# A two-block transformer kernel on one core: hi/lo operands side by side, and a turned triangular inverse

## The reference

```python
h = rms_norm(x, norm_mix_pre); proj = h @ w_in
o_sb = stick_breaking_attention(q, k, v); o_rw = rwkv7_time_mix(p_rw, ...)
merged = gates[..., :D] * (o_sb @ w_sb_out) + gates[..., D:] * (o_rw @ w_rw_out)
x = x + rms_norm(merged @ w_o, norm_mix_post)
h = rms_norm(x, norm_ffn_pre)
x = x + rms_norm((silu(h @ w_ffn_gate) * (h @ w_ffn_up)) @ w_ffn_down, norm_ffn_post)
# second block
x = x + hybrid_mixer(rms_norm_2(x, g_mix), w_in, conv_w, ...)
x = x + memory_cross_attention(rms_norm_2(x, g_xattn), rms_norm_2(mem, g_mem), ...)
x = x + squared_relu_mlp(rms_norm_2(x, g_mlp), w_up, w_down)
out = rms_norm_2(x, g_final)
```

## Time and profile before

| what | value |
|---|---|
| median of three runs | 852.21 us |
| the profiled execution, its own time | 853.91 us |
| its span in the trace | 852.0 us |
| mean granted clock of TensorE | 0.995 |
| busy: PE, DVE, ACT | 839.8, 546.1, 394.4 us |
| mean DMA rate | 165 GB/s |

### The profile page before, as it was taken

One profiled execution on the slowest core, in us unless ns is written; L12 is line 12 of the kernel. 1 busy time (PEld: TensorE's weight loads), 2 busy tenths in 40 slices (PEclk: granted clock), 3 DMA queues, 4 the chain that ended last, 5 costly groups with the idle time before them and its releaser, 6 DMA issues.

```text
span 852.0 us, 16571 instructions
## 1 busy us (share of the span) xinstructions
PE 839.8 (99%) x7276; PEld 773.3 (91%) x7276; DVE 546.1 (64%) x606; ACT 394.4 (46%) x457; POOL 5.9 (1%) x8
## 2 busy tenths in 40 slices
PE   9999999999999999999999999999999999999997
PEld 8989889898989999999999989988998999999996
DVE  5998755546788655555557656595754765566554
ACT  6652331366367434343447354446544533344432
POOL 0000010000000000000000000000000000000000
PEclk9998999999999999999999999999999999999999
DMA  9845513131674665646553754536433465555531
GB/s 299 282 150 177 167 54 102 54 99 53 241 244 132 198 199 196 194 151 200 194 198 100 246 170 136 175 124 206 176 103 123 140 228 174 180 193 183 178 133 49
DMA packets 97002, 140.62 MB, mean 165 GB/s; under 512 B 2480, under 2 KB 79408, under 8 KB 96944
## 3 DMA queue, kind: packets, MB, share of 16 engines
q1 hardware_dynamic: 96512, 139.36, 50.0%
q10 hardware_dynamic: 432, 0.39, 0.2%
HBM read 138.69 MB, written 1.05 MB: 164 GB/s over the span
## 4 chain that ended last, share of the span: by engine, by line
PE 88%; DVE 6%; ACT 2%; issue 2%; DMA 2%; SPq 0%; ACTq 0%; DVEq 0%
PE PS L427 86%; DMA raw<-in_w_in_dram 2%; DVE wlo L1627 2%; PE PS L530 1%; ACT whi L1201 1%; DVE rw L1689 1%; DVE diff L1686 0%; DVE stg L1684 0%; DVE Gm L1781 0%; ACT st L1201 0%; PE PS L673 0%; PE PS L1037 0%; DVE cs L1706 0%; DVE wlo L1664 0%; DVE krs L1719 0%
## 5 line engine op out<-in xcount | busy, mean ns | idle before, releaser
L1627 DVE TENSOR_TENSOR wlo<-raw,whi 128x2048 fp32r<-128x2048 f32 x122 | 279.4, 2291 | 136.8 <-ACT whi L1201 136.5
L1201 ACT ACTIVATE whi<-raw 128x2048 fp32r<-128x2048 f32 (+1 forms) x130 | 241.2, 1858 | 181.3 <-PE PS L427 177.7
L427 PE MATMUL PS<-xh,whi 128*128 128x256 f32 x1136 | 322.4, 287 | 0.9 <-ACT xh L1201 0.7
L427 PE MATMUL PS<-xh,wlo 128*128 128x256 f32 x1136 | 317.2, 284 | 0.1
L427 PE MATMUL PS<-xl,whi 128*128 128x256 f32 x1136 | 315.2, 284 | 0.0
L427 PEld LDWEIGHTS PS<-xh,whi 128*128 128x128 f32 x1136 | 217.9, 193 | 5.9 <-issue 3.3
L427 PEld LDWEIGHTS PS<-xh,wlo 128*128 128x128 f32 x1136 | 217.2, 193 | 0.3 <-DVE wlo L1664 0.3
L427 PEld LDWEIGHTS PS<-xl,whi 128*128 128x128 f32 x1136 | 215.7, 193 | 1.1
L427 PE MATMUL PS<-whi,fh 128*128 128x512 f32 x216 | 84.4, 391 | 0.0
L427 PE MATMUL PS<-wlo,fh 128*128 128x512 f32 x216 | 84.4, 391 | 0.0
L427 PE MATMUL PS<-whi,fl 128*128 128x512 f32 x216 | 84.1, 389 | 0.0
(11 more groups left out here) (310 smaller groups left out, 1045.0 us busy)
## 6 DMA issues: line engine op xcount, KB each, us to landing
raw<-in_w_in_dram SPq DMA_DIRECT2D x32, 1024.0 KB, 5.3
raw<-in_w_up_dram SPq DMA_DIRECT2D x16, 1024.0 KB, 5.3
raw<-in_w_down_dram SPq DMA_DIRECT2D x16, 1024.0 KB, 4.9
raw<-in_w_ffn_gate_dram SPq DMA_DIRECT2D x11, 1024.0 KB, 5.3
raw<-in_w_ffn_up_dram SPq DMA_DIRECT2D x11, 1024.0 KB, 5.4
raw<-in_w_ffn_down_dram SPq DMA_DIRECT2D x11, 1024.0 KB, 5.0
raw<-in_w_kv_mem_dram SPq DMA_DIRECT2D x8, 1024.0 KB, 5.4
raw<-in_w_o_dram SPq DMA_DIRECT2D x4, 1024.0 KB, 8.0
```

The lines of the kernel that those rows point to most:

```text
L427: return nc.tensor.matmul(o, l, r, start=start, stop=stop, **kw)
L1201: return nc.scalar.activation(o, i, f, **kw)
L1627: V.tensor_tensor(wlo[u % RING][:], raw[u % RING][:], whi[u % RING][:].bitcast(f32), ALU.subtract) \
```

## The change

`xh` and `xl` lie side by side for each k in one tile `xhl` (and `memhl`), so that one matmul can stream both: 512 columns. In 63 of the units by features (`by_feature_wide`: 4 of `U_QK`, 8 of `U_G`, 2 of `U_KM`, 20 of the first feed-forward, 3 of `U_QK2`, 8 of `FILL2`, 3 of `U_QM`, 15 of the last feed-forward), a tile f is 8 matmuls `whi` with `xhl` of 512 columns, then 8 matmuls `wlo` with `xh` of 256 columns. The left half of a bank holds whi*xh + wlo*xh, the right half whi*xl; a unit fills two banks. ACT copies the right halves out (`second_halves`, by unit, or by tile in `FILL2` and `U_QM`), DVE adds the left halves (`summed`), and then multiplies by the norm factors in SBUF. The units of the stages `U_QK`, gates, `FILL2` and `U_QM` use fewer bank pairs than before; the gate units all use banks 0 and 1 and wait for the sum of the unit before.

The inverse no longer updates `TT` by a product. `join` forms only the update of `Tm`, `lower` streams only the 32 columns that the level needs, and a new `turned(v)` forms the new columns of `TT` by a matmul of `Tm` with the identity (32 columns), which DVE copies out in `lower_out` of the next level. The pairs and transposes that stood between (`pairs(eN, eX)`, `tokens(rw, 8)`) use banks 6 and 7, and the products behind the inverse change their order.

The maximum and reciprocal of `krs` move ahead of the eight instructions that end in `k_mod`.

```diff
+            def by_feature_wide(u, both, banks, later=0, before=None, between=None, amidst=None, first=None):
+                n = units[u][1]
+                wh, wl = split(u, n, later)
+                for f in range(2):
+                    if before:
+                        before(f)
+                    fs = slice(f * P, (f + 1) * P)
+                    o = bank(banks[f])
+                    for k in range(KD):
+                        if amidst:
+                            amidst(f, k)
+                        mm(o, wh[:, k, fs], both[:, k].rearrange("p a t -> p (a t)"), k == 0, False, skip_group_check=True)
+                    for k in range(KD):
+                        last = mm(o[:, 0:SEQ], wl[:, k, fs], both[:, k, 0], False, k == KD - 1, skip_group_check=True)
...
             def lower(v):
+                n = HD // 2
                 pe.wait_ge(sem("t_ready"), v)
-                pe.wait_ge(sem("tt_ready"), v)
-                for c, tt, s_, h, b, l, r in out_of(lambda c, tt, s_: XT[half(c), c ^ tt, s_, :], lambda c, tt, s_: Tm[half(c), c ^ tt, s_, :]):
-                    last = mm(PS[h, b * 512 + s_ * HD:b * 512 + (s_ + 1) * HD], l, r, True, True)
+                if v == 1:
+                    pe.wait_ge(sem("tt_ready"), 1)
+                else:
+                    turned(v - 1)
+                if v == 6:
+                    return
+                for c, tt, s_, h, b, l, r in out_of(lambda c, tt, s_: XT[half(c), c ^ tt, s_, :],
+                                                    lambda c, tt, s_: halves(Tm[half(c), c ^ tt, s_, :], v, 0)):
+                    last = mm(PS[h, b * 512 + s_ * n:b * 512 + (s_ + 1) * n], l, r, True, True)
                 last.then_inc(sem("g_mm"), 1)
+            def turned(v):
+                n = HD // 2
+                for c, tt, s_, h, b, l, r in out_of(lambda c, tt, s_: Tm[half(c), c ^ tt, s_, :],
+                                                    lambda c, tt, s_: halves(C("ident")[half(c), half(c)], v, 1)):
+                    last = mm(PS[h, b * 512 + 256 + s_ * n:b * 512 + 256 + (s_ + 1) * n], l, r, True, True)
+                last.then_inc(sem("turn_mm"), 1)
...
             def gate_unit(i):
                 before(i)
-                pe.wait_ge(sem("out_evac"), i + 10)
-                by_feature(U_G[i], xh, xl, (i + 11) % 2, None, lambda f: amid(i))
+                if i == 0:
+                    pe.wait_ge(sem("summed"), halved("qk", 4))
+                else:
+                    pe.wait_ge(sem("summed"), halved("gate", i))
+                by_feature_wide(U_G[i], xhl, (0, 1), between=lambda: amid(i))
                 behind(i)
...
+            def second_halves(dst, banks):
+                return A_(dst, tiles(banks)[:, :, 1], ACT.Copy)
...
+            def summed(dst, banks):
+                return V.tensor_tensor(dst, tiles(banks)[:, :, 0], dst, ALU.add)
...
                 if i == 5:
+                    dve.wait_ge(sem("kk_sd"), 1)
+                    link(V.tensor_scalar(krs[:], krs[:], 1e-12, None, ALU.max))
+                    V.reciprocal(krs[:], krs[:]).then_inc(sem("kk_rs"), 1)
+                if i == 5:
                     for j in range(NPAIR):
...
-                if i == 5:
-                    dve.wait_ge(sem("kk_sd"), 1)
-                    link(V.tensor_scalar(krs[:], krs[:], 1e-12, None, ALU.max))
-                    V.reciprocal(krs[:], krs[:]).then_inc(sem("kk_rs"), 1)
...
             def mlp(i, n=0):
                 later = FF2_BODY * n
+                if i:
+                    act.wait_ge(sem("units_used"), U_M["u", i] + 1 + FF2_STEP * n)
+                    if i >= 2:
+                        act.wait_ge(sem("mlp_hi"), i - 1 + later)
+                        act.wait_ge(sem("mlp_sq"), i - 1 + later)
+                    second_halves(pair(fa[i % 2]), MLP_BANKS[i % 2]).then_inc(sem("mlp_second"), 1)
```

More of the change, by code:

```diff
@@ L249, in bank, with halved, tiles @@
             return PS[:, b * 512:(b + 1) * 512]
+        HALVED = {"qk": 4, "gate": 8, "km": 2, "qk2": 3, "fill": 16, "qm": 6}
+        def halved(kind, n):
+            return sum(HALVED[o] for o in list(HALVED)[:list(HALVED).index(kind)]) + n
+        def tiles(banks):
+            a, b = banks
+            return PS[:].rearrange("p (b h t) -> p b h t", b=8, h=2)[:, a:b + 1:b - a]
         def C(name):
@@ L712, in join @@
             def join(v):
                 pe.wait_ge(sem("g_ready"), v)
+                pe.wait_ge(sem("tt_ready"), v)
                 n = HD // 2
[L715 to L728, removed]
+                for c, tt, s_, h, b, l, r in back_to(lambda c, tt, s_: TT[half(c ^ tt), c, s_, :],
+                                                     lambda c, tt, s_: halves(Gm[half(c ^ tt), c, s_, :], v, 0)):
+                    last = mm(PS[h, b * 512 + s_ * n:b * 512 + (s_ + 1) * n], l, r, True, True)
@@ new lines, in behind @@
+            def behind(i):
+                if i == 0:
+                    pe.wait_ge(sem("pair_ready"), 1)
+                    pairs(eX, kk, "pair_mm")
+                elif i < 6:
+                    join(i)
+                    if i in (2, 3):
+                        pe.wait_ge(sem("pair_ready"), 4)
+                        pe.wait_ge(sem("tok_ready"), i - 1)
+                        for j in range(NPAIR):
+                            last = nc.tensor.transpose(PS[:, 7 * 512 + j * P:7 * 512 + (j + 1) * P],
+                                                       rw[:, 8 + j, (i - 2) * P:(i - 1) * P], C("ident"))
+                        last.then_inc(sem("tok_T"), 1)
+                elif i == 6:
@@ L2119, in mem_queries @@
             def mem_queries(i):
-                dve.wait_ge(sem("units_used"), U_QM[i] + 1)
-                V.tensor_tensor(qm[:, 2 * i:2 * i + 2, :], two(i % 2 if i else 2), spread(rs), ALU.mult).then_inc(sem("qm_evac"), 1)
+                if i == 0:
+                    dve.wait_ge(sem("units_used"), U_QM[i] + 1)
+                    V.tensor_tensor(qm[:, 0:2, :], two(2), spread(rs), ALU.mult).then_inc(sem("qm_evac"), 1)
+                    return
+                for f in range(2):
+                    dst = qm[:, 2 * i + f, :]
+                    dve.wait_ge(sem("second"), halved("qm", 2 * i + f - 1))
+                    V.tensor_tensor(dst, bank(f)[:, 0:SEQ], dst, ALU.add).then_inc(sem("summed"), 1)
+                    dve.wait_ge(sem("summed"), halved("qm", 2 * i + f - 1))
+                    last = V.tensor_tensor(dst, dst, rs, ALU.mult)
+                last.then_inc(sem("qm_evac"), 1)
             dve.wait_ge(norm_sem("n4", "rs"), nth("n4", "rs", 1))
```

358 lines of the change are left out of this document (230 added, 128 removed).

## The result

The changed kernel takes 841.79 us (median of four executions, 841.16 to 842.34) where the kernel before took 852.23 us beside it: ratio 0.9878, 95% interval 0.986 to 0.9895. It is 10.4 us faster. The forecast was 835.2 us, so the sign was right and 6.6 us of the 17.0 are missing; the time also lies above the range's end of 841.

The account below looks back on a forecast made before the run. PE's own stream was taken to bound the kernel. Wide operand 10.6 + inverse 4.7 + stretch up to the gate stage 2.3 - new waits 0.6 = 17.0 us off the median 852.21: 835.2 us, range 832.5 to 841.

Parts of the forecast that it names:

- Term 1: Wide units: fewer, wider matmuls save 0.18 us a unit; 59 units behind the first stage give 10.6 us (10.0 to 12.4).
- deduction for changes of width: Wide units: about two more narrow-to-wide changes a unit at 0.02 us each, 0.04 us off the saving.
- best case of 0.21 us a unit: Wide units: sixteen pairs of 768 columns, each 0.347 us instead of 0.360, save 0.21 us a unit.
- Term 2: Inverse: three 32-column blocks a level replace the old products, 14.4 us instead of 19.2; 4.7 us taken as saving.
- Term 4: New waits on added copies and sums, gate stage, state part and feed-forwards: mostly covered, 0.6 us lost.
- Term 3: Up to the gate stage: krs wait and slow clock go, DVE's gn_pre then limits; 2.3 us earlier (1.5 to 3).
- signs that the prediction had named: Trace marks for each part: matmul distances, block times, clock and logits start, PE's waits on copies and sums under 2 us.
- (B): Before the gate stage: PE's 2 us stand drops the clock, costing 1.7 to 3.4 us; 838 us, chance 0.25.
- (C): Inverse: bound by its chain over DVE, so shorter matmuls only lengthen waits and its saving is lost; 840 us, chance 0.09.
- (D): Wide units: fixed cost per matmul is not saved, gain 2.4 us or less; 843 to 846 us, chance 0.06.
- (E): Loops: weight supply turns late behind the added copy and add, kernel slower; 860 us at 1 us per turn, chance 0.05.
- (F): Whole kernel: losses from new waits add up to the whole gain; 851 to 854 us, chance 0.03.

Follow-up runs that it names:

- x4: The changed kernel with each 512-column matmul of the wide units issued as two of 256 columns, copies and sums kept: 853.55 us, ratio 1.0007.
- x7: x3 with wide and narrow matmuls in turn for each k, 32 changes of width a unit instead of 4: 839.84 us.
- x6: x3 with the inverse of the kernel before, its pairs and transposes back in their old places and banks: 841.87 us.
- x1: The changed kernel with DVE's key_sum set ahead of the lo that stood before it, for both key units: 836.85 us, ratio 0.981.
- x8: The kernel before once more, unchanged, for a second trace: 852.51 us over 12 executions, the traced one 852.32 us.
- x5: The kernel before with only the maximum and reciprocal of krs moved ahead of the k_mod instructions: 850.58 us, ratio 0.9976.
- x9: The changed kernel once more, unchanged, for a second trace and more executions: 841.34 us, ratio 0.9868.
- x2: The changed kernel with DVE's lo for a gate unit's weights moved behind the group norm preparations: 840.47 us, ratio 0.9858.
- x3: The changed kernel with both the edit of x1 and the edit of x2: 835.05 us, ratio 0.9786.

## Why the prediction was wrong, point by point

- **What bounds the kernel:** right. PE sets the pace, and removing its instructions moved the time.
- **Term 1, the wide operand:** right in mechanism and near in size. x4 gives 11.8 us for the 63 units against 11.3 forecast; that 2.0 us of it are stalls and 1.0 us is hidden by waits makes the match of the medians partly luck, but 0.191 us a unit in the last feed-forward is free of both. A turn of the last feed-forward takes (822.05 - 689.73) / 12 = 11.03 us (the starts of two down units, twelve turns apart), as forecast. The deduction for changes of width was too large (x7), and the best case of 0.21 us a unit was not reached either. Between the parts of dilated attention and of memory attention the units saved only 0.10 and 0.07 us in place of 0.18. The trace of x4 splits this: narrow matmuls cost 1.07 and 0.33 us there (0.13 and 0.11 a unit), and x4, which has the added copies and sums without the saving, takes 0.29 and 0.13 us more than before.
- **Term 2, the turned inverse:** right in sum for a partly wrong reason. The whole is worth 5.5 to 6.8 us (x6), forecast 4.7. The products give 3.7 of it and not 4.8, the shorter waits for `Gm` 1.5, and 0.5 is a stall that no wait explains. Term 4 had put the inverse's waits at 0.2 us more; they became less. It also had 0.4 us more for `St`, whose waits stayed at 0.5 us.
- **Term 3, up to the gate stage:** the start at 94.50 was forecast at 95.3, the wait for `gn_pre` at 2 and measured at 1.75 us. The size of the clock's share was right where it happened: 3.1 us forecast, 3.05 measured between two traces of the same kernel. The sum of DVE's work and idle time was 0.8 us too pessimistic.
- **Term 4, new waits: this is the step that failed.** It sums the new waits to a loss of 0.6 us. It names the gate stage, the state part and both feed-forwards, and finds, in the feed-forwards, a whole unit of 5.5 us between a sum and the reuse of its banks. `U_KM[1]` and the second unit of `U_QK2` share banks 0 and 1 with one narrow unit between them, and the sum stands in DVE's list behind a `lo` of 2.29 us for which ACT must first round. Both facts are in the code, and the copy at 271.05 is of the same tile `km`, from `U_KM[0]`. Only the boundary between the two stages wasn't walked through. Forecast 0, measured 4.5 to 4.9 us (x1): 2.94 us of standing, 0.1 of handover and 1.5 of slow clock in the traces. Of the signs that the prediction had named, the one that failed is waits on copies and sums under 2 us in all.
- **The sum's transfer to the median: the second step that failed.** The text takes 17.0 us off the profiled execution "and equally off the median". The clock's fall at `krs`, 3.05 us, was in the profiled execution, while the traced execution next to the median (852.32, x8) had another, of 1.5 us, elsewhere. So 1.7 us of term 3 had no counterpart in the median, and x5 shows it: 3.8 us between the profiled executions, 1.8 between the medians. With 0.6 us in which the changed kernel's own profiled execution lies below its median this is the 2.3 us between 12.7 and 10.4.
- **The rivals:** (B) feared a fall of the clock behind the new stand of 1.75 us at the gate stage. There was none in either trace of the changed kernel (clock 1.00 from 93 to 101 us); it fell behind the stand that wasn't foreseen. Of its price, 1.7 to 3.4 us, the lower end (half of 3.5 us of slow clock) stands on no row of the prediction; the falls measured cost 1.5 to 3.05. (C) fell with x6, (D) with x4, although their times of 840 and 843.4 lie nearer to the 841.79 measured than the forecast does. (E), a late weight supply in the loops, didn't appear: the last feed-forward's turn is as forecast, with no wait. (F), no gain at all, is out with the result.

## What to carry to other kernels

When a buffer's release gets one more step on another engine, go through every pair of neighbours that use the buffer, at the boundaries of stages above all, and read in the releasing engine's list what stands ahead of the release; a cheap release behind someone else's 2.3 us of work cost the critical engine 4.5 to 4.9 us here, and exchanging two lines gave it back. A loss that one profiled execution shows, a slow clock above all, is to be scaled by how far that execution's own time lies from the median, before it is booked as a gain. Fewer, wider matmuls were worth what the distance of their starts said.

## What the runs showed of the hardware

- The granted clock falls in some executions and not in others behind the same wait of the same program: 1.18 us (0.50 in the first trace of before, 1.00 in x8), 0.83 and 0.84 us (1.00 in the first, 0.50 in x8). Behind the wait of 2.94 us it fell to 0.50 in three traces (after, x4, x9) and stayed at 1.00 in one (x2), and in the four traces in which this wait is gone (x1, x3, x6, x7) there is no fall. A fall cost 3.05, 1.5 and 1.5 us. One fall (x8) stands behind a wait as short as 0.84 us, which the prediction had excluded ("waits of 0.8 us dropped nothing"); that this wait brought it about isn't shown.
- A change of width between neighbouring matmuls is nearly free, under 0.003 us (x7). A block of 64 instructions on 64x64 tiles with 32 columns (`lower`, `turned`, `join`) takes 0.96 us when another such block follows and 1.07 us ahead of 128-row matmuls (rows of the timeline after, above), while the update of `TT` in the kernel before, with equal columns, took 1.97 us; why was not tested.
